# Linear attention beside a projection: the seven levels of a chunk in four TensorE visits in place of seven

## What is computed

```python
def step(state, inp):
    qb, kb, vb, gb = inp
    cum = jnp.cumsum(gb, axis=-2)
    diff = cum[..., :, None, :] - cum[..., None, :, :]
    decay = jnp.exp(jnp.where(causal, diff, -jnp.inf))
    scores = jnp.einsum('bhtd,bhsd,bhtsd->bhts', qb, kb, decay)
    o_intra = jnp.einsum('bhts,bhsv->bhtv', scores, vb)
    o_inter = jnp.einsum('bhtd,bhdv->bhtv', qb * jnp.exp(cum), state)
    total = cum[..., -1, :]
    k_dec = kb * jnp.exp(total[..., None, :] - cum)
    new_state = jnp.exp(total)[..., None] * state + jnp.einsum('bhsd,bhsv->bhdv', k_dec, vb)
    return new_state, o_intra + o_inter
```

## Time and profile before

| | us |
|---|---|
| median of 3 runs | 2454.61 (2453.95 to 2457.71) |
| profiled execution, its own time | 2452.28 |
| its span, first to last instruction | 2450.6 |
| TensorE busy (share of the span) | 2372.3 (97%) |
| VectorE busy | 1538.1 (63%) |
| POOL busy | 1165.5 (48%) |
| ScalarE busy | 846.1 (35%) |
| mean granted TensorE clock | 0.989 of full |

### The profile page before, as it was taken

How to read it: one execution, slowest core, us unless ns; L and a number is a source line. 1 busy time by engine, 2 the same in 40 slices (tenths; PEclk the granted TensorE clock), 3 DMA queues, 4 the chain that set the end, 5 groups by cost and what they waited for, 6 DMA issues and landing times.

```text
span 2450.6 us, 33556 instructions
## 1 busy us (share of the span) xinstructions
PE 2372.3 (97%) x12578; PEld 1931.4 (79%) x12578; DVE 1538.1 (63%) x1926; ACT 846.1 (35%) x1288; POOL 1165.5 (48%) x659
## 2 busy tenths in 40 slices
PE   7999999999999899999999999999999999999996
PEld 5777877888888688778877787788877888788885
DVE  6777878876611761113157767645798666777788
ACT  4555464432200221252023223222263333343444
POOL 4375667663434553233223323333464555566664
PEclk9999999999999999999999999999999999999998
DMA  5313333336111322122222222232134444853322
GB/s 209 129 75 137 122 125 107 133 128 242 43 51 49 122 96 70 48 104 74 85 78 82 64 77 81 66 99 83 60 121 145 162 161 142 293 225 133 130 91 81
DMA packets 126655, 277.38 MB, mean 113 GB/s; under 512 B 11713, under 2 KB 56001, under 8 KB 121938
## 3 DMA queue, kind: packets, MB, share of 16 engines
q1 hardware_dynamic: 84544, 216.04, 25.4%
q10 hardware_dynamic: 42002, 59.87, 7.1%
HBM read 199.26 MB, written 76.61 MB: 113 GB/s over the span
## 4 chain that ended last, share of the span: by engine, by line
PE 60%; DVE 9%; issue 3%; DMA 2%; ACT 2%; POOL 1%; SPq 0%; DVEq 0%; ACTq 0%; POOLq 0%
PE pt L2650 32%; PE pt L3103 14%; PE wk L3103 6%; PE pt L2666 1%; DMA eb<-o_d 1%; PE wk L3015 1%; PE wk L3114 1%; DVE darg L2190 1%; POOL xl L711 1%; DVE eb L2272 1%; PE wk L2985 1%; PE wk L3053 1%; PE wk L3048 1%; PE wk L3049 1%; PE wk L2937 0%
## 5 line engine op out<-in xcount | busy, mean ns | idle before, releaser
L676 POOL TENSOR_TENSOR w_hi<-w_raw,ones 128x1024 fp32r<-128x1024 f32 x94 | 181.9, 1935 | 752.9 <-PE pt L2650 711.2
L680 POOL TENSOR_TENSOR w_lo<-w_raw,w_hi 128x1024 fp32r<-128x1024 f32 x104 | 279.4, 2686 | 83.6 <-ACT w_hi L931 60.7
L2650 PE MATMUL pt<-h,w_hi 128*128 128x512 f32 x896 | 289.7, 405 | 1.8 <-ACT cu_o L1309 1.8
L2650 PE MATMUL pt<-l,w_hi 128*128 128x512 f32 x896 | 277.5, 391 | 0.0
L2650 PE MATMUL pt<-h,w_lo 128*128 128x512 f32 x896 | 277.1, 390 | 0.0
L2650 PEld LDWEIGHTS pt<-l,w_hi 128*128 128x128 f32 x896 | 168.8, 188 | 36.3
L2650 PEld LDWEIGHTS pt<-h,w_lo 128*128 128x128 f32 x896 | 168.6, 188 | 36.2
L2650 PEld LDWEIGHTS pt<-h,w_hi 128*128 128x128 f32 x896 | 161.1, 189 | 37.9 <-ACT ebuf L1304 5.3
L796 POOL TENSOR_TENSOR wr_l<-raw,wr_h 128x512 fp32r<-128x512 f32 x80 | 137.1, 1719 | 81.0 <-ACT wr_h L1451 81.0
L738 POOL TENSOR_TENSOR xl<-sraw,xh 128x512 fp32r<-128x512 f32 x80 | 135.8, 1707 | 83.3 <-ACT xh L998 83.3
L796 POOL TENSOR_TENSOR wr_l<-fraw,wr_h 128x512 fp32r<-128x512 f32 x60 | 79.2, 1323 | 92.6 <-ACT wr_h L1451 92.6
(11 more groups left out here) (577 smaller groups left out, 6096.3 us busy)
## 6 DMA issues: line engine op xcount, KB each, us to landing
w_raw<-ws_d SPq DMA_DIRECT2D x106, 512.0 KB, 3.3
fx_d<-stg SPq DMA_DIRECT2D x106, 256.0 KB, 2.7
sraw<-ws_d SPq DMA_DIRECT2D x32, 512.0 KB, 5.9
fraw<-ws_d SPq DMA_DIRECT2D x32, 512.0 KB, 4.8
raw<-ws_d SPq DMA_DIRECT2D x32, 512.0 KB, 9.1
xs0f<-fx_d SPq DMA_DIRECT2D x10, 1024.0 KB, 5.2
xs1f<-fx_d SPq DMA_DIRECT2D x9, 1024.0 KB, 5.0
xs2f<-fx_d SPq DMA_DIRECT2D x9, 1024.0 KB, 4.9
```

The lines of the kernel that those rows point to most:

```text
L676: nc.gpsimd.tensor_tensor(out=w_hi[:, u, :], in0=w_raw[:, u, :], in1=zeros, op=ALU.add).then_inc(w_hi_done, 1)
L680: nc.gpsimd.tensor_tensor(out=w_lo[:, u, :], in0=w_raw[:, u, :], in1=w_hi[:, u, :].bitcast(f32), op=ALU.subtract).then_inc(w_split, 1)
L2650: ins = MM(pt[:, slot, h * HALF:(h + 1) * HALF], wt[:, k * P:(k + 1) * P], x[:, k, h * HALF:(h + 1) * HALF], start=first and k == 0 and n ...
```

## The change

The levels are visited in four places in place of seven. After step 3 of the first tile TensorE does levels 0 and 1, after step 6 levels 2 and 3; in the second tile levels 4 and 5 follow step 5 and level 6 follows step 7. The matmuls, their number, the semaphores and the programs of the other engines stay as they are.

```diff
@@ -3026,12 +3026,16 @@
                         ins.then_inc(dg_mm, 1)
                     if k == 1:
                         pe.wait_ge(oc_done, i)
-                    if k in (3, 5, 7):
-                        level((k - 3) // 2)
+                    if k in (3, 6):
+                        level((k - 3) // 3 * 2)
+                        level((k - 3) // 3 * 2 + 1)
 
                 def in_r(k):
-                    if k in (1, 3, 5, 7):
-                        level(3 + (k - 1) // 2)
+                    if k == 5:
+                        level(4)
+                        level(5)
+                    if k == 7:
+                        level(6)
                     if k == 6:
                         pe.wait_ge(kd_done, i + 1)
                         for h in range(GH):
```

## The result

| | before | after |
|---|---|---|
| median (us) | 2454.28 of 6 runs | 2474.60 of 6 runs |
| lowest and highest | 2451.56 to 2457.71 | 2471.62 to 2475.97 |
| profiled execution | 2452.28 | 2475.36 |
| granted TensorE clock, mean | 0.989 | 0.982 |

The account below looks back on a forecast made before the run. TensorE, busy 97% of the span, was taken to set the pace. Wait less saving +10.0 us and clock +7.0 give +17 on 2452.3, 2469; with 2.3 us from execution to median, 2471.5 us, range 2462 to 2477.

Parts of the forecast that it names:

- The wait at level 1: Between levels 0 and 1, TensorE idles 2.23 us for VectorE's kp in seven chunks, not in the first.
- the delay moves along with TensorE: VectorE's chain starts from TensorE's progress 10 us before, so the 2.23 us wait returns in every chunk but the first.
- The saving: Three of seven visits fewer, and no wait before level 4: about 0.7 us saved a chunk, 5.6 over eight.
- the joint inside a visit: Passing between two levels of one visit: bounded by 0 and 0.23 us, taken as 0.05 us each.
- a full seam: Leaving and entering a visit on TensorE costs 0.23 us beyond the work.
- The wait ahead of level 4: Between levels 3 and 4, TensorE waits 0.14 us for VectorE; the changed order removes it.
- Levels 3, 4, 5 and 6: Later visits in the chunk: no wait for VectorE, about 1 us in hand at levels 4 and 5.
- The clock: TensorE falls to 1.2 GHz behind five of seven new waits, 1.4 us each, +7.0 us.
- The sum: Chunks 1 to 7 +10.7 us, chunk 0 -0.7, clock +7.0: total +17 us.
- A: The forecast case: wait at level 1, clock falling in four to seven chunks, 2470 to 2475 us; chance 0.58.
- B: Same wait at level 1, clock stays or falls in at most three chunks: 2464.6 to 2469 us; chance 0.28.
- C: Level 1 ready when level 0 is done, in every chunk: only the saving, -5.6 us, 2449 us; chance 0.04.

Follow-up runs that it names:

- e2_pairs_later: The changed kernel with levels 0 and 1 after step 5, levels 2 and 3 after step 7 of the first tile: 2444.57 us, 2444.69 when repeated.
- e3_wait_filled: The changed kernel with nine unread 128x512 matmuls put between levels 0 and 1: 2466.54 us.
- e11_three_fillers: The changed kernel with three unread 128x512 matmuls put between levels 0 and 1: 2466.51 us.
- e5_short_w_lo: The changed kernel with POOL computing only the first 64 columns of w_lo in the loop's 24 tiles, the rest left out: 2449.49 us.
- e10_kdt_joins: The kernel of e2_pairs_later with the transposes of kd moved into the visit after step 5 of the second tile, behind level 5: 2446.00 us.
- e8_pairs_at_4_and_6: The changed kernel with levels 0 and 1 after step 4, levels 2 and 3 after step 6 of the first tile: 2453.47 us.
- e1_first_pair_apart: The changed kernel with level 0 after step 3 and level 1 after step 5 of the first tile, other pairs kept: 2447.27 us.
- e4_vectore_reordered: The changed kernel with level 1's two multiplies directly after level 0's in VectorE's program, kd's argument behind the diagonal's copy: 2448.37 us.

## Why the prediction came true, point by point

**The wait at level 1: right in place, size and count.** Predicted 2.23 us in seven chunks and none in the first; measured 2.12 of idle time, and 2.80 - 0.58 = 2.22 us later start. Its cause was named rightly in both halves: VectorE's order (taking level 1 forward removes all but some 0.2 us of it) and POOL's operation (cutting it short takes 2.1 us off the argument). That the delay moves along with TensorE held in every chunk.

**The saving: the direction right, its size too small.** The step that failed is the bound of the joint inside a visit, "by 0 and by a full seam", with 0.05 us taken. It can lie below zero: in the first chunk two levels together are 0.15 us (0 and 1) and 0.08 us (2 and 3) shorter than apart and 0.09 us (4 and 5) longer, 0.14 less in all where 0.15 more was forecast. No reason for excluding a gain was given. The wait ahead of level 4 was sized on one chunk, too: it is 0.14 us there, but 0.24 in the first and every second one, where it has a row of its own:

```profile
1259.25 0.73 PE L2650 MATMUL pt<-h,w_hi 128*128 128x512 f32 x2
...
1262.44 0.44 PE L3015 MATMUL wk<-qc,kp 128*32 128x16 f32 x32 [0.18 <-DVE kp L2204]
```

1262.44 - 1259.25 = 3.19 us, against 2.95 without a wait. Together 0.69 + 0.14 + 0.24 = 1.07, and 45.41 - 44.32 = 1.1 us were saved where 0.7 were forecast. e2_pairs_later, where nothing waits, gives 45.3 - 43.9 = 1.4 us a chunk: 1.1 and the 0.2 to 0.3 of level 0.

**Levels 3, 4, 5 and 6: right.** No idle time ahead of any; `kp` 5 had 1.3 us in hand against 1 forecast. The transfers played no part.

**The clock: right that it falls, too low in price and count.** Five falls at 1.4 us were forecast, a part of each slow stretch inside the wait. In the trace it fell in all seven, 0.2 us before the end of the wait at the earliest, so that next to nothing of the slow stretch was hidden; it cost about 1.5 us by e3_wait_filled, and 3.1 in one chunk. The count of five rested on two idle times; the same two places of the program, in all eleven traces, have twelve of 1.88 to 2.33 us, and the clock fell at nine or within 2 us behind them. So after an idle time of this length it may fall or not.

The Trainium skill (TensorE: Matmul & The Clock Gate, "Why this matters for your kernels") ties the fall to longer idle gaps. That didn't hold for this wait: 2.12 us were enough seven times. Of the shorter ones, seven of 1.02 to 1.12 us and three of 1.44 to 1.46 us did nothing, and one of seven of 1.21 to 1.24 us took the clock down. What decides it beside the length stays open.

**The sum.** From the first level 0 to the last (seven intervals) the trace has 334.41 us against 317.21, 17.2 more, and the last chunk 2.8 more: 20.0 in the loop. What wait and saving make of it shows e11_three_fillers, where level 1 starts equally late at a full clock: 46.5 us a chunk, 1.2 more than before. It is 2.22 - 1.0 and not 2.22 - 1.1, since a visit with a wait in it doesn't gain the 0.15 us of levels 0 and 1 back to back. So 7 x 1.2 - 1.1 = 7.3 us, where 10.0 were forecast; the other 12.7 are the clock's, where 7.0 were (six times 48.1 - 46.5 = 1.6, and once 3.1). The two errors partly cancelled, and that is luck: 17 against 20. What is left between the two profiled executions, 23.1 - 20.0 = 3.1 us, lies outside the loop, where the programs are the same. Executions differ there: the idle time that took 2.33 us in rows 11 took 3.95 in the changed kernel's trace, with about 6.8 us at 1.2 GHz from there on:

```profile
192.67 1.97 PE L2837 MATMUL wk<-ident,st 128*128 128x128 f32 x8 [3.95 <-DMA st<-xbc_d]
```

**The rivals.** A is the case that came. B (level 1 as late, full clock) is what e11_three_fillers (but for one fall) and e3_wait_filled show: 10 to 12 us above the kernel before on their chips. C's premise was tried in e5_short_w_lo: with the collision gone the median is 6.3 us below the kernel before (1 to 7 by its interval), where C had 5.6. That it fits is chance: level 1 was not ready, waits of 0.4 to 1.5 us stayed, and the loop gave only 2.3 us of it. The 2.2 us were not the only distance.

## What to carry to other kernels

Before small work is gathered into fewer visits, look up for each piece when its producer finishes, and not only what the visit costs: here a pair was worth 1.1 us a chunk and one operand 2.2 us late. The same gathering with its first visit two steps later was the fastest kernel tried (with e10_kdt_joins, which these runs can't tell from it), so first move the visit, then judge the idea. Price an idle time of the matrix engine with what follows it: of each wait's 3.7 us, some 1.5 came from the slow clock after it had ended. And judge a loop by the distance of its own instructions, since the rest of the program varies between executions, here by up to 10 us ahead of the loop.

## What was not expected of the hardware

- In the loop the clock fell at seven of seven idle times of 2.12 us (the change), at none of three of 1.44 to 1.46 us (e5_short_w_lo), at one of seven of 1.21 to 1.24 us (e11_three_fillers, after three filling matmuls) and at none of seven of 1.02 to 1.12 us (e8_pairs_at_4_and_6); it was then at 1.2 GHz for about 3.4 us, once for 6.8.
- At two waits for a DMA outside the loop it fell at nine of twelve idle times of 1.88 to 2.33 us, or within 2 us behind them, over eleven traces of a stretch that no edit touches.
- Useless matmuls in a wait paid here: three of them, 0.68 us of a wait that was there anyway, took 8 us off the kernel.
- Small matmuls of two levels back to back can take less than their sum: 1.05 us for 0.61 + 0.59, and 0.68 for 0.38 + 0.38. Not always: levels 2 and 3 took 0.78 to 0.80 us in e1_first_pair_apart and 0.84 to 0.89 in e4_vectore_reordered but for its first chunk.
